# Chunks of the first half of the first gated layer in engine loops, and a wait for the delta scan's state signal written ahead of the first merge chunk's load

## Chip, core and metric

The kernel runs on one core of one Trainium2 chip. The metric is the device time of one execution in microseconds (us), as the median of several executions. Lower is better.

## The reference, cut to what matters

Two blocks run one after the other on 528 tokens (16 meta tokens and 512) of width 1024. The part that the change touches is the first of the two gated layers of the first block, and a load in its mixing part:

```python
for l in range(DEPTH):                                   # DEPTH = 1
    h = h + 0.5 * swiglu(rmsnorm(h, ffn1_norm[l]), ffn1_w_gate[l], ffn1_w_up[l], ffn1_w_down[l])
    u = rmsnorm(h, mix_norm[l])
    (c_q, c_kv, k_rope, g_q, g_k, g_v, g_b, g_a, g_z,
     gate_mla, gate_gdn) = jnp.split(u @ w_in[l], split_points, axis=-1)
    y_mla = mla(...) @ w_mla_o[l]
    y_gdn = gated_deltanet(...) @ w_gdn_o[l]             # a scan over 9 chunks of 64 tokens with a state
    merged = jax.nn.sigmoid(gate_mla) * y_mla + jax.nn.sigmoid(gate_gdn) * y_gdn
    h = h + merged @ w_out[l]
    h = h + 0.5 * swiglu(rmsnorm(h, ffn2_norm[l]), ...)

def swiglu(x, w_gate, w_up, w_down):                     # hidden width D_FF = 2816
    return (jax.nn.silu(x @ w_gate) * (x @ w_up)) @ w_down
```

A second block, an attention layer of three branches, follows and is not touched.

## The kernel before, in words

All large weights come through one stream of chunks. A chunk is up to 128 x 2048 numbers (1 MB); `STREAM` lists the runs of chunks by name, and `n` numbers them through the whole kernel. `RAW`, `WHI` and `WLO` have two slots each, and chunk n uses slot n % 2. Each engine has its own part of the work on a chunk and its own program:

- SyncE (SP) loads chunk n into `RAW` (L592) once `lo_rdy` (printed as weights_lo_ready) says that the slot's chunk before, n - 2, is split.
- ScalarE (ACT) makes the rounded part, `WHI` (L1540), of chunk n + 1 while TensorE multiplies chunk n.
- VectorE (DVE) makes the rest, `WLO` = `RAW` - `WHI` (L2123), of chunk n + 1.
- TensorE (PE) multiplies: for each block three products, `WHI` by the high part of the tokens, `WLO` by the high part, `WHI` by the low part (L743, L744, L745), 264 columns each.
- VectorE and ScalarE turn the result into the hidden layer: DVE `SILU` (L2349), ACT `TANH` (L1676), DVE `SILU` (L2351), DVE `GF` (L2356, which frees the PSUM banks: `evac`), DVE `GF` (L2359), ACT `GH` (L1678), DVE `GL` (L2361).

A gated layer f runs in two halves of 11 hidden blocks. "f1u0" is the gate and up product of the first half of the first layer (11 chunks, numbers 0 to 10), "f1d0" its down product (8 chunks), then "f1u1" and "f1d1". In f1u0 one chunk is 96 matmuls on TensorE (8 x 2 x 2 x 3), in f1d0 it is 66. Two PSUM halves alternate: the matmuls of chunk n wait until chunk n - 2 is read (`evac` at n - 1) and until `WLO` of chunk n is there.

The function `stream(eng, name, body, straight, first)` writes one engine's program for a run. With `straight=True` each chunk's instructions are written out. Otherwise `first` chunks (2 if it is the kernel's first run) are written out, the next ones stand once, two chunks per pass, in a loop of the engine (`eng.Fori`, L406), and what is left over is written out. In a loop the chunk number `n` that the body gets is not a Python integer but an expression over the loop's register, so every semaphore count and address that depends on it is computed by register instructions, and a test such as `isinstance(n, int)` is false. That f1d0 stands in a loop on TensorE and SyncE, and that f2u0, f2d0, f2u1, the second layer's runs, and the merge chunks "mg" stand in loops, is so before and after.

The merge chunks: "mg" is a run of 16. SyncE's program for it starts at its first chunk in a loop (first=0: seven passes of two, two chunks written out). The delta scan is the loop over `NCH` = 9 chunks behind L2860; `st_rdy` is its semaphore, raised by 2 at L2861 when the state is cleared, and by one for each half of a new state. Engines take the waits of their own program in order: what stands behind a waiting instruction on an engine waits too.

The functions that the diff touches, and what calls them:

Of the kernel before, what the change touches and what calls it, by code (L numbers as in the profile page):

```python
# [49 lines left out]
START = {}  # L50
# [29 lines left out]
def build(nc, io):  # L80
# [216 lines left out]
    def halves(ap):  # L297
# [39 lines left out]
    st_rdy, ws_ps, vn_rdy, sa_ps, o_ps, o_ev = (sem(x) for x in (  # L337
        "state_ready", "ws_in_psum", "v_new_ready", "state_add_in_psum", "delta_o_in_psum",
        "delta_o_ready"))
# [42 lines left out]
    def chunk_width(name, parity):  # L382
        if name == "mg":
            return SLOT if parity == 0 else SLOT // 2
        return WIDTH[name]

    def stream(eng, name, body, straight=False, first=0):

        n0, count = START[name], COUNT[name]
        at_ = ORDER.index(name)
        after = chunk_width(ORDER[at_ + 1], 0) if at_ + 1 < len(ORDER) else 0
        head = 2 if n0 == 0 else first

        def one(j):
            n = n0 + j
            body(n, j, n // 2, n % 2, chunk_width(name, (j + 1) % 2) if j + 1 < count else after)

        if straight:  # L400
            head = count
        for j in range(head):
            one(j)
        trips = (count - head - 1) // 2
        if trips > 1:
            with eng.Fori(0, trips) as i:  # L406
                for s in range(2):
                    n = n0 + head + s
                    body(2 * i + n, 2 * i + head + s, i + n // 2, n % 2,
                         chunk_width(name, (head + s + 1) % 2))  # L410
            done = head + 2 * trips
        else:
            done = head
        for j in range(done, count):
            one(j)
# [156 lines left out]
    @block.sync  # L572
    def _(sp):
        sp.dma_start(COL[:, :], io["cols"]).then_inc(col_ld, 16)
        for i in range(2):
            sp.dma_start(first_half(RAW, i), io["f1u0"][0].rearrange("p (a b) -> p a b", a=2)[
                :, :, i * KD // 2 * P:(i + 1) * KD // 2 * P]).then_inc((w0_ld, raw_ld[0])[i], 16)
        load_h(sp, 1)
        sp.dma_start(TAB[:, 0:TABS["cos"]], io["tabs"][:, 0:TABS["cos"]]).then_inc(ones_ld, 16)

        def load(name):
            def body(n, j, turn, slot, nxt):
                if isinstance(n, int) and n == 0:
                    return
                if isinstance(n, int) and n - 2 in SEVEN:
                    sp.wait_ge(p_lo, 7 * SEVEN[n - 2] + 7)
                elif not isinstance(n, int) or n >= 2:
                    sp.wait_ge(lo_rdy, n)
                w = chunk_width(name, (n - START[name]) % 2 if isinstance(n, int) else
                                (slot - START[name]) % 2)  # L590
                src = io[name][j] if name != "mg" else io["mg"][j, :, 0:w]
                sp.dma_start(RAW[:, slot, 0:w], src).then_inc(raw_ld[slot], 16)  # L592
                if isinstance(n, int) and n == 1:
                    sp.dma_start(RELB[:, :], io["rel"]).then_inc(tab_ld, 16)
                    sp.dma_start(TAB[:, TABS["cos"]:], io["tabs"][:, TABS["cos"]:]).then_inc(tab_ld, 16)
            return body

        def spread_rows():

            sp.wait_ge(gt_d, 6)  # L600
            sp.dma_start(io["rows"][0], RW[B8, 0, :]).then_inc(row_st, 16)
            sp.dma_start(io["rows"][1], RW[A8, 1, :]).then_inc(row_st, 16)
            sp.wait_ge(row_st, 32)
            for i, (t, landed) in enumerate(((EU, kx_ld), (QX, qx_ld))):
                if i:
                    sp.wait_ge(kn_ps, 4)
                for p in range(2):
                    sp.dma_start(pair_rows(t)[CH * p:CH * (p + 1), :, :],
                                 bass.AP(io["rows"].tensor, (NH * i + p) * NROW, [[0, CH], [2 * NROW, 4], [1, NROW]]))\
                        .then_inc(landed, 16)  # L610

        for name in ORDER[:-1]:
            stream(sp, name, load(name), straight=name in ("f1u0", "f1u1"), first=2 if name in ("f1d0", "f1d1") else 0)
            if name == "z":
                spread_rows()
        n0 = START["wo2"]
        for j in range(2):
            load("wo2")(n0 + j, j, 0, (n0 + j) % 2, 0)

        for j in range(2, 4):  # L620
            load("wo2")(n0 + j, j, 0, (n0 + j) % 2, 0)
        for j in range(4):
            sp.wait_ge(evac, n0 + j + 1)
            sp.dma_start(io["out"][2 * j:2 * j + 2].rearrange("k p t -> p k t"),
                         H[:, 2 * j:2 * j + 2, N_META:T1]).then_inc(out_st, 16)
        sp.wait_ge(out_st, 64)
# [111 lines left out]
    def _(pe):  # L738
# [109 lines left out]
        def ffn(f, c0, w):  # L848
            hi, lo = parts(3 * f)
            gh, gl = hidden(f)  # L850
            for half in range(2):
                def up(n, j, turn, slot, nxt):
                    if isinstance(n, int) and n == 0:
                        warm_up()
                        first_chunk(hi, lo)
                        return
                    if seven(n):
                        seven_products(n)
                        if ends_run(n):
                            pe.sem_inc(mm_done, n + 1 - SEVEN_FIRST[n])  # L860
                        return
                    pe.wait_ge(lo_rdy, n + 2)
                    if not isinstance(n, int) or n >= 2:
                        pe.wait_ge(evac, n - 1)
                    if isinstance(n, int) and n == START["f2u0"] + 1:

                        pe.wait_ge(rstd_rdy, TURN[3])
                    for k in range(KD):
                        pe.wait_ge(ul_rdy, KD * ROUND[3 * f] + k + 1)
                        if isinstance(n, int) and (n, k) in ((1, 3), (START["f2u0"], 3)):  # L870
                            square_sums(3 * f)
                        for which in range(2):
                            for b, (a, m, c) in enumerate(pieces(w)):
                                last = mm3(PS[:, 4 * slot + 2 * which + b, c:c + m], slot,
                                           (which * KD + k) * P, hi[:, k, a:a + m], lo[:, k, a:a + m],
                                           k == 0, k == KD - 1)
                    last.then_inc(mm_done, 1)

                def down(n, j, turn, slot, nxt):
                    pe.wait_ge(lo_rdy, n + 2)  # L880
                    pe.wait_ge(evac, n - 1)
                    if last_down(f, half, j):
                        down_by_halves(n, slot, gh, gl)
                        return
                    for k in range(FHALF):
                        pe.wait_ge(gl_rdy, (2 * f + half) * FHALF + k + 1)
                        for b, (a, m, c) in enumerate(pieces(w)):
                            last = mm3(PS[:, 4 * slot + b, c:c + m], slot, k * P, gh[:, k, a:a + m],
                                       gl[:, k, a:a + m], k == 0, k == FHALF - 1)
                    last.then_inc(mm_done, 1)  # L890

                if f == 0 and half == 1:
                    pe.wait_ge(rev_rdy, 1)
                stream(pe, f"f{f + 1}u{half}", up, straight=f == 0, first=2)
                if f == 0 and half == 0:
                    relative_rows()
                stream(pe, f"f{f + 1}d{half}", down, first=0 if f else 2)
# [326 lines left out]
        for g in range(NB // SIDE):  # L1224
            for lv in range(LEVELS):
                for x in range(SIDE):
# [10 lines left out]
                    for r in range(UB):  # L1237
                        u = (SIDE * g + x) * UB + r
# [9 lines left out]
                for x in range(SIDE if lv else 0):  # L1248
# [4 lines left out]
                    for r in range(UB):  # L1253
                        u = b * UB + r
# [8 lines left out]
            for x in range(SIDE):  # L1263
# [3 lines left out]
                for r in range(UB):  # L1267
                    u = b * UB + r
# [101 lines left out]
        n = START["wv"]  # L1370
# [130 lines left out]
        n = START["wt"]  # L1501
# [26 lines left out]
    def _(act):  # L1528
# [125 lines left out]
        def ffn(f, c0, w):  # L1654
            TANH, SILU, GF = staging(f)
            for half in range(2):
# [31 lines left out]
                        act.wait_ge(evac, n + 1)  # L1688
                        high(1, j)

                stream(act, f"f{f + 1}u{half}", up, straight=f == 0, first=2)
                stream(act, f"f{f + 1}d{half}", down, straight=f == 0 or half == 1)

        def only_weights(n, j, turn, slot, nxt):
# [69 lines left out]
        n = START["uq"]  # L1764
# [151 lines left out]
        n = START["z"]  # L1916
# [63 lines left out]
        n = START["wv"]  # L1980
# [128 lines left out]
    def _(dve):  # L2109
# [216 lines left out]
        def ffn(f, c0, w):  # L2326
            gh, gl = hidden(f)
            TANH, SILU, GF = staging(f)
            for half in range(2):
# [58 lines left out]
                        if f == 0:  # L2388
                            low(1, j)

                stream(dve, f"f{f + 1}u{half}", up, straight=f == 0, first=0 if half else 2)
                if f == 0 and half == 0:
                    dve.wait_ge(rev_ps, 1)
                    TS(REV, PS[0:16, 7, 0:383], -1.0, None, ALU.mult).then_inc(rev_rdy, 1)
# [939 lines left out]
```

## Time and profile before

| | |
|---|---|
| time of three runs, median | 1569.19 us (1568.25 to 1571.32) |
| time of the profiled execution | 1561.85 us |
| its span, first to last instruction | 1560.2 us |
| mean granted TensorE clock | 0.993 of full |
| TensorE busy | 1524.6 us (98%) |
| VectorE busy | 955.0 us (61%) |
| ScalarE busy | 593.9 us (38%) |

The profile is of one execution, by the hardware's own records. PE stands for TensorE's matmuls, PEld for its weight loads, which overlap them; DVE is VectorE, ACT ScalarE, POOL GpSimd, SP SyncE. A q behind an engine's name is its sequencer, the part that waits, branches, computes registers and issues transfers; its instructions are not counted as busy. L743 is line 743 of the kernel. In a row of the timeline the first number is the start in us from the span's start, the second the duration; brackets give the engine's idle time before and what ended it.

### The profile page before, as it was taken

Reading aid. Unit: us, or ns where it says so; the run is one execution under the profiler, and the core shown is the slowest. Engines: PE = TensorE matmul, PEld = TensorE weight load, DVE = VectorE, ACT = ScalarE, POOL = GpSimd, SP = SyncE. Lnnn points to the kernel's source line nnn. Section 1 sums busy time; section 2 is a strip of 40 time slices with the busy share of each in tenths; the row PEclk is TensorE's granted clock in tenths of the full one; section 3 lists DMA queues with packets and bytes.
Section 4 is the critical chain, followed back from the end, with each engine's and each line's share of the span. In section 5 each row is a group of like instructions: output and inputs, shape, how many; then the busy total and the mean of one; then the engine's idle time right before and its main releaser. Section 6 shows DMA issues by size and latency. Waiting matters only on the chain.

```text
span 1560.2 us, 30264 instructions
## 1 busy us (share of the span) xinstructions
PE 1524.6 (98%) x12676; PEld 1338.6 (86%) x12676; DVE 955.0 (61%) x1528; ACT 593.9 (38%) x968; POOL 127.6 (8%) x124
## 2 busy tenths in 40 slices
PE   9999999999999999999999989999999989999998
PEld 8999999999997789988888878888888877776777
DVE  6546588855389776555445666634666565557872
ACT  6222356632255562042232322222322144446960
POOL 0000000000001640500000000000000000000410
PEclk9999999999999999999999999999999999999999
DMA  6222223246332200012224243433442353211001
GB/s 242 82 101 75 96 96 109 92 116 150 95 76 69 62 3 31 4 43 75 100 81 164 93 162 121 137 103 125 149 147 81 101 217 135 71 52 55 2 10 73
DMA packets 27683, 147.92 MB, mean 95 GB/s; under 512 B 2928, under 2 KB 3328, under 8 KB 16944
## 3 DMA queue, kind: packets, MB, share of 16 engines
q1 hardware_dynamic: 21616, 122.50, 22.9%
q0 software_dynamic: 5424, 22.68, 5.4%
q8 instruction: 88, 1.44, 0.4%
q10 hardware_dynamic: 528, 1.08, 0.2%
q14 instruction: 27, 0.22, 0.0%
HBM read 140.97 MB, written 5.27 MB: 94 GB/s over the span
## 4 chain that ended last, share of the span: by engine, by line
PE 90%; DVE 4%; ACT 3%; issue 1%; DMA 1%; DVEq 0%; SPq 0%; ACTq 0%; POOLq 0%
PE PS L743 22%; PE PS L744 22%; PE PS L745 22%; PE PS L843 2%; PE PS L845 2%; PE PS L844 2%; PE PS L1260 1%; PE PS L1195 1%; PE PS L1245 1%; PE PS L1155 1%; PE PS L1068 1%; PE PS L1258 1%; ACT PB L1898 1%; PE PS L779 1%; PE PS L1169 1%
## 5 line engine op out<-in xcount | busy, mean ns | idle before, releaser
L1540 ACT ACTIVATE WHI<-RAW 128x2048 fp32r<-128x2048 f32 (+3 forms) x113 | 189.4, 1676 | 277.6 <-PE PS L745 273.6
L2123 DVE TENSOR_TENSOR WLO<-RAW,WHI 128x2048 fp32r<-128x2048 f32 (+3 forms) x113 | 225.9, 1999 | 66.1 <-ACT WHI L1540 65.3
L743 PE MATMUL PS<-UH,WHI 128*128 128x264 f32 (+1 forms) x736 | 227.6, 309 | 2.1 <-DVE WLO L2123 2.1
L744 PE MATMUL PS<-UH,WLO 128*128 128x264 f32 (+1 forms) x736 | 226.3, 307 | 0.0
L745 PE MATMUL PS<-UL,WHI 128*128 128x264 f32 (+1 forms) x736 | 226.0, 307 | 0.0
L743 PE MATMUL PS<-UHS,WHI 128*128 128x512 f32 x520 | 205.5, 395 | 5.2 <-DVE WLO L2123 5.2
L745 PE MATMUL PS<-ULS,WHI 128*128 128x512 f32 x520 | 203.4, 391 | 0.0
L744 PE MATMUL PS<-UHS,WLO 128*128 128x512 f32 x520 | 203.3, 391 | 0.0
L743 PEld LDWEIGHTS PS<-UH,WHI 128*128 128x128 f32 x736 | 139.2, 189 | 9.1 <-DVE WLO L2123 2.5
L744 PEld LDWEIGHTS PS<-UH,WLO 128*128 128x128 f32 x736 | 139.2, 189 | 6.4 <-issue 0.2
L745 PEld LDWEIGHTS PS<-UL,WHI 128*128 128x128 f32 x736 | 138.9, 189 | 6.3
L743 PEld LDWEIGHTS PS<-UHS,WHI 128*128 128x128 f32 x520 | 98.3, 189 | 27.7 <-issue 7.1
L745 PEld LDWEIGHTS PS<-ULS,WHI 128*128 128x128 f32 x520 | 98.2, 189 | 20.8
L744 PEld LDWEIGHTS PS<-UHS,WLO 128*128 128x128 f32 x520 | 98.4, 189 | 20.0 <-issue 0.2
L744 PE MATMUL PS<-GH,WLO 128*128 128x264 f32 x352 | 100.2, 285 | 0.0
L745 PE MATMUL PS<-GL,WHI 128*128 128x264 f32 x352 | 100.0, 284 | 0.0
L743 PE MATMUL PS<-GH,WHI 128*128 128x264 f32 x352 | 99.8, 284 | 0.0
L1676 ACT ACTIVATE TANH<-SILU 128x512 f32<-128x512 f32 (+1 forms) x33 | 21.0, 637 | 191.4 <-DVE SILU L2349 191.4
L843 PE MATMUL PS<-FH,WHI 128*128 128x264 f32 x308 | 87.8, 285 | 0.1
L845 PE MATMUL PS<-FL,WHI 128*128 128x264 f32 x308 | 87.3, 283 | 0.0
L844 PE MATMUL PS<-FH,WLO 128*128 128x264 f32 x308 | 87.2, 283 | 0.0
L2381 DVE SCALAR_TENSOR_TENSOR H<-PS,H 128x528 f32<-128x528 f32 (+2 forms) x31 | 21.6, 697 | 96.1 <-PE PS L745 96.1
(474 smaller groups left out, 3256.2 us busy)
## 6 DMA issues: line engine op xcount, KB each, us to landing
RAW<-in_f2u SPq DMA_DIRECT2D x22, 1024.0 KB, 4.9
RAW<-in_f1u SPq DMA_DIRECT2D x21, 1024.0 KB, 4.8
ADA<-in_ada POOLq DMA_DIRECT2D x24, 512.0 KB, 4.8
RAW<-in_f1d SPq DMA_DIRECT2D x16, 704.0 KB, 4.1
RAW<-in_f2d SPq DMA_DIRECT2D x16, 704.0 KB, 4.1
RAW<-in_wi SPq DMA_DIRECT2D x10, 1024.0 KB, 4.9
RAW<-in_w SPq DMA_DIRECT2D x8, 1024.0 KB, 5.1
RAW<-in_mg SPq DMA_DIRECT2D x8, 1024.0 KB, 4.9
```

The lines of the kernel that those rows point to most:

```text
L743: mm(out, WHI[:, slot, c:c + w], hi, start=first, stop=False)
L744: mm(out, WLO[:, slot, c:c + w], hi, start=False, stop=False)
L745: return mm(out, WHI[:, slot, c:c + w], lo, start=False, stop=last)
L779: out = mm(PS[:, 2 * which + b, c:c + m], stationary[:, 0, (which * KD + k) * P:(which * KD + k + 1) * P], moving[:, k, a:a + m], start=fi ...
L843: mm(out, whi[:, ks], hi, start=starts and k == 0, stop=False, skip_group_check=True)
L844: mm(out, wlo[:, ks], hi, start=False, stop=False, skip_group_check=True)
L845: last = mm(out, whi[:, ks], lo, start=False, stop=ends, skip_group_check=True)
L1068: last = mm(scores(i, p, k0, k1), q, KH[0:96, h, k0:k1], start=True, stop=True)
L1540: A(WHI[:, slot, 0:w], RAW[:, slot, 0:w], ACT.Copy).then_inc(hi_rdy, 1)
L1676: A(TANH[:, slot, 0:w], SILU[:, slot, 0:w], ACT.Tanh, scale=0.5).then_inc(tanh_rdy, 1)
L2123: TT(WLO[:, slot, 0:w], RAW[:, slot, 0:w], WHI[:, slot, 0:w].bitcast(f32), ALU.subtract).then_inc(lo_rdy, 1)
L2381: STT(h, psum(4 * slot, w), 0.25, h, ALU.mult, ALU.add)\
```

## The change

Two edits. In SyncE's load of a chunk a wait for `st_rdy` >= 2 is added under the condition that the chunk number is an integer and is that of the first merge chunk. And the run f1u0 is no longer straight on SyncE, TensorE, ScalarE and VectorE; f1u1 stays straight.

```diff
@@ load(name) of SyncE
                 elif not isinstance(n, int) or n >= 2:
                     sp.wait_ge(lo_rdy, n)
+                if isinstance(n, int) and n == START["mg"]:
+                    sp.wait_ge(st_rdy, 2)
                 w = chunk_width(name, (n - START[name]) % 2 if isinstance(n, int) else
@@ SyncE
-            stream(sp, name, load(name), straight=name in ("f1u0", "f1u1"), first=2 if name in ("f1d0", "f1d1") else 0)
+            stream(sp, name, load(name), straight=name == "f1u1", first=2 if name in ("f1d0", "f1d1") else 0)
@@ TensorE
-                stream(pe, f"f{f + 1}u{half}", up, straight=f == 0, first=2)
+                stream(pe, f"f{f + 1}u{half}", up, straight=f == 0 and half == 1, first=2)
@@ ScalarE
-                stream(act, f"f{f + 1}u{half}", up, straight=f == 0, first=2)
+                stream(act, f"f{f + 1}u{half}", up, straight=f == 0 and half == 1, first=2)
@@ VectorE
-                stream(dve, f"f{f + 1}u{half}", up, straight=f == 0, first=0 if half else 2)
+                stream(dve, f"f{f + 1}u{half}", up, straight=f == 0 and half == 1, first=0 if half else 2)
```

The lines behind L588 move by two in the changed kernel. How the programs of three engines change:

SyncE, at the start of the merge chunks, in the changed kernel (RAW<-in_mg is the load of a merge chunk; QX<-rows is a transfer of the delta part, ahead of it):

```order
L610 DMA QX<-rows 64x4x576
L406 UNCONDITIONAL_BRANCH
L406 ISA
L594 ISA [waits weights_lo_ready]
L594 DMA RAW<-in_mg 128x2048
L588 REGISTER_ALU
L594 ISA [waits weights_lo_ready]
L594 DMA RAW<-in_mg 128x1024
L406 REGISTER_ALU
L406 COMPARE_AND_BRANCH
```

The rows of before are these same ten with L592 for L594 and L608 for L610. The loads wait for weights_lo_ready alone in both.

TensorE in f1u0, the edge between chunks 1 and 2, before:

```order
L744 MATMUL PS<-UH_79,WLO 128x264
L745 MATMUL PS<-UL_80,WHI 128x264
L743 MATMUL PS<-UH_79,WHI 128x264 [waits normed_lo_ready,chunk_evacuated,weights_lo_ready]
L744 MATMUL PS<-UH_79,WLO 128x264
L745 MATMUL PS<-UL_80,WHI 128x264
```

and in the changed kernel (the edge, then the end of the loop's body and the first matmul of chunk 10 behind it):

```order
L747 MATMUL PS<-UL_80,WHI 128x264
L406 UNCONDITIONAL_BRANCH
L406 ISA
L866 REGISTER_ALU [waits weights_lo_ready]
L745 MATMUL PS<-UH_79,WHI 128x264 [waits normed_lo_ready,chunk_evacuated]
...
L406 REGISTER_ALU
L406 COMPARE_AND_BRANCH
L745 MATMUL PS<-UH_79,WHI 128x264 [waits normed_lo_ready,chunk_evacuated,weights_lo_ready]
```

The matmuls and their waits are the same; a branch and register instructions stand at the edge, and the 192 matmuls of two chunks, with as many weight loads, stand between the loop's head and its branch.

VectorE in f1u0, one chunk as it stands written out for each of chunks 2 to 10 before:

```order
L2123 TENSOR_TENSOR WLO<-RAW,WHI 128x2048 [waits chunk_multiplied,weights_hi_ready]
L2349 TENSOR_TENSOR SILU_74<-PS,KEEP 128x528 [waits hidden_ready,rstd_ready,chunk_multiplied]
L2351 SCALAR_TENSOR_TENSOR SILU_74<-TANH_73,SILU_74 128x528 [waits tanh_ready]
L2356 TENSOR_TENSOR GF_75<-SILU_74,PS 128x528 [waits hidden_lo_ready,silu_ready]
L2359 TENSOR_TENSOR GF_75<-GF_75,KEEP 128x528 [waits chunk_evacuated]
L2361 TENSOR_TENSOR GL<-GF_75,GH 128x528 [waits hidden_hi_ready]
```

and the loop's first chunk in the changed kernel:

```order
L406 ISA
L492 REGISTER_ALU [waits weights_hi_ready]
L2125 TENSOR_TENSOR WLO<-RAW,WHI 128x2048 [waits chunk_multiplied]
L2346 REGISTER_ALU
L2349 REGISTER_ALU [waits rstd_ready,chunk_multiplied]
L2351 TENSOR_TENSOR SILU_74<-PS,KEEP 128x528 [waits hidden_ready]
L2353 SCALAR_TENSOR_TENSOR SILU_74<-TANH_73,SILU_74 128x528 [waits tanh_ready]
L2358 TENSOR_TENSOR GF_75<-SILU_74,PS 128x528 [waits hidden_lo_ready,silu_ready]
L2361 TENSOR_TENSOR GF_75<-GF_75,KEEP 128x528 [waits chunk_evacuated]
L2363 ISA [waits hidden_hi_ready]
L2363 TENSOR_TENSOR GL<-GF_75,GH 128x528
```

The six operations of a chunk keep their order; a register instruction or a wait of its own stands ahead of some of them.

## Rows read from the trace of the kernel before

**Rows 1.** The page: busy time, the chain that ended last, the instruction queue.

```profile
PE 1524.6 (98%) x12676; PEld 1338.6 (86%) x12676; DVE 955.0 (61%) x1528; ACT 593.9 (38%) x968; POOL 127.6 (8%) x124
...
q8 instruction: 88, 1.44, 0.4%
...
PE 90%; DVE 4%; ACT 3%; issue 1%; DMA 1%; DVEq 0%; SPq 0%; ACTq 0%; POOLq 0%
```

**Rows 2.** Busy time by windows: f1u0 and f1d0 (window us, busy us, instructions).

```profile
21.20:138.40 117.20, 117.20 (x971) 116.92 (x969) 61.86 (x63) 34.66 (x36) 0.00 (x0) 1.00 0.26 90
139.30:203.90 64.60, 64.60 (x532) 64.60 (x533) 40.39 (x45) 20.36 (x21) 6.25 (x2) 1.00 0.26 89
```

**Rows 3.** All waits of weight loads, 21.2 to 204 us (total us, times, longest).

```profile
PEld PS L743 <- issue: 0.6, 1, 0.6
PEld PS L766 <- issue: 0.2, 1, 0.2
```

**Rows 4.** Timeline of VectorE in f1u0, one chunk.

```profile
45.87 0.71 DVE L2349 TENSOR_TENSOR SILU<-PS,KEEP 128x528 f32<-128x528 f32 x1 [3.17 <-PE PS L745]
...
50.20 0.71 DVE L2361 TENSOR_TENSOR GL<-GF,GH 128x528 fp32r<-128x528 f32 x1 [0.71 <-ACT GH L1678]
52.01 2.29 DVE L2123 TENSOR_TENSOR WLO<-RAW,WHI 128x2048 fp32r<-128x2048 f32 x1 [1.10 <-ACT WHI L1540]
57.46 0.71 DVE L2349 TENSOR_TENSOR SILU<-PS,KEEP 128x528 f32<-128x528 f32 x1 [3.16 <-PE PS L745]
```

**Rows 5.** Timeline of ScalarE in f1u0, the same chunk.

```profile
46.61 0.65 ACT L1676 ACTIVATE TANH<-SILU 128x528 f32<-128x528 f32 x1 [6.23 <-DVE SILU L2349]
49.52 0.65 ACT L1678 ACTIVATE GH<-GF 128x528 fp32r<-128x528 f32 x1 [2.26 <-DVE GF L2359]
50.07 1.90 ACT L1540 ACTIVATE WHI<-RAW 128x2048 fp32r<-128x2048 f32 x1
```

**Rows 6.** Timeline of VectorE in f2u1, in a loop before and after.

```profile
1102.53 0.69 DVE L2349 TENSOR_TENSOR SILU<-PS,RSTD 128x512 f32<-128x512 f32 x1 [1.32 <-PE PS L745]
...
1107.07 0.69 DVE L2361 TENSOR_TENSOR GLS<-GF,GHS 128x512 f32 x1 [0.93 <-ACT GHS L1678]
1108.75 2.29 DVE L2123 TENSOR_TENSOR WLO<-RAW,WHI 128x2048 fp32r<-128x2048 f32 x1 [0.99 <-ACT WHI L1540]
```

**Rows 7.** Sequencers at the loops' line, whole kernel, then 150 to 190 us.

```profile
L406 SPq COMPARE_BRANCH  x34: 40/45/54, 146.4 to 1334.1; - x34
L406 PEldq COMPARE_BRANCH  x25: 76/208/240, 169.3 to 1230.4; - x25
L406 DVEq COMPARE_BRANCH  x18: 50/56/68, 741.8 to 1183.3; - x18
L406 ACTq COMPARE_BRANCH  x17: 40/45/54, 741.0 to 1182.5; - x17
...
L406 PEldq COMPARE_BRANCH  x2: 76/158/240, 169.3 to 185.4; - x2
```

**Rows 8.** DMA queue of TensorE's instructions (packets, MB, share): 155 to 187, 21 to 139 us.

```profile
q8 instruction: 1, 0.02, 0.2%
...
q8 instruction: 7, 0.11, 0.4%
```

**Rows 9.** DMA issues: KB each, us from issue to landing.

```profile
RAW<-in_f1u SPq DMA_DIRECT2D x21, 1024.0 KB, 4.8
RAW<-in_mg SPq DMA_DIRECT2D x8, 1024.0 KB, 4.9
COL<-in_cols SPq DMA_DIRECT2D x1, 94.0 KB, 2.3
```

**Rows 10.** Timelines around the delta scan: SyncE, VectorE, ScalarE.

```profile
599.07 115.65 SPq L592 DMA_DIRECT2D RAW<-in_mg  x4
...
660.89 0.27 DVE L2860 MEMSET SV<- 128x256 f32 x1
...
682.70 1.90 ACT L1540 ACTIVATE WHI<-RAW 128x2048 fp32r<-128x2048 f32 x1
```

**Rows 11.** Timeline of TensorE in f2u0 behind an idle stretch.

```profile
919.71 0.77 PE L743 MATMUL PS<-UHS,WHI 128*128 128x512 f32 x1 [5.25 <-DVE WLO L2123]
920.27 0.63 PE L744 MATMUL PS<-UHS,WLO 128*128 128x512 f32 x1
920.70 0.63 PE L745 MATMUL PS<-ULS,WHI 128*128 128x512 f32 x1
...
925.38 0.39 PE L744 MATMUL PS<-UHS,WLO 128*128 128x512 f32 x1
925.61 0.40 PE L745 MATMUL PS<-ULS,WHI 128*128 128x512 f32 x1
```

**Rows 12.** The same place by windows: the clock stands behind the counts.

```profile
919.60:925.80 6.20, 6.09 (x15) 4.84 (x16) 4.38 (x7) 2.17 (x3) 0.53 (x1) 0.54 0.71 254
925.80:935.00 9.20, 9.20 (x42) 7.59 (x41) 4.12 (x4) 1.49 (x2) 0.53 (x1) 1.00 0.48 171
```

## The prediction, made before the changed kernel was run

> **What bounds the kernel.** I read the page first. TensorE is busy for 98% of the span, and 90% of the chain that ended last is TensorE's own work [rows 1]. So a change counts only where it delays or hastens a matmul. Then I looked at the stretch that the change rewrites. In the 117.20 us of f1u0 TensorE is busy for all 117.20 us, at full clock, through 971 instructions, which is 0.121 us for each [rows 2]. One chunk of 96 matmuls is therefore 11.6 us. The list of waits says the same from the other side: over f1u0 and f1d0 the weight loads wait 0.6 us and 0.2 us, once each, and for no other engine [rows 3]. The reader is to see that f1u0 is a pure TensorE stretch, in which the other three engines have slack. The question is how much slack, and what a loop costs against it.
>
> **The first edit, the wait.** Its condition asks for an integer chunk number. SyncE takes the merge chunks from the first one in a loop, where the number is an expression over a register, so the condition is false when the program is written. The listing in the section on the change bears this out: the load of the first merge chunk waits for weights_lo_ready alone, as before. Cost 0, because nothing is added.
>
> I also price the case that it were there. The first merge load is issued at 599.07 us. The signal comes when the state is cleared, at 660.89 + 0.27 = 661.2 us. ScalarE first reads the chunk at 682.70 us [rows 10]. The load would land 4.9 us behind its issue [rows 9], at 666.1 us, 16.6 us before it is wanted. Behind it on SyncE stand only later merge loads, which wait for this chunk to be split. So a real wait would cost 0 too.
>
> **The second edit, TensorE.** Chunks 2 to 9 become four passes of two chunks; chunks 0, 1 and 10 stay written out. Added are a loop entry and, per pass, register instructions and a branch, of which three are taken. A taken branch on TensorE's sequencer takes about 0.21 to 0.24 us, one that falls through 0.076 us [rows 7]. The nearest stretch that already is a loop on TensorE is f1d0, with the same matmul shape. It spends 64.60 us of 64.60 us busy on 532 instructions, again 0.121 us each [rows 2], and the list of waits has no entry for its edges [rows 3] (the 0.6 us stands before f1d0's first matmul, at the one small matmul of the relative rows). What hides the branch there is that the sequencer is ahead of the array: it branched back at 169.3 us [rows 7], while the matmuls of four chunks, 4 x 66 x 0.121 = 32.0 us from 139.3 us, end at 171.3 us. That is 2.0 us ahead. Branch and register work of perhaps 0.4 us per pass fit into it. Cost 0; without that cover it would be 4 x 0.4 = 1.6 us.
>
> **VectorE.** In f1u0 one chunk on VectorE runs from `SILU` at 45.87 us to the end of `WLO` at 52.01 + 2.29 = 54.30 us, and then VectorE is idle for 3.16 us until TensorE has finished [rows 4]. `WLO` of the next chunk is thus ready 3.2 us before TensorE can use it. What do the register instructions cost? The second layer's f2u1 runs the same operations in a loop. From the start of `SILU` to the end of `GL` it takes 1107.07 + 0.69 - 1102.53 = 5.23 us [rows 6], against 50.20 + 0.71 - 45.87 = 5.04 us written out [rows 4]. From the start of `GL` to the start of `WLO` it is 1.68 us [rows 6] against 1.81 us [rows 4]. So a loop costs 0.2 us per chunk, and with the branch of 0.056 us [rows 7] at most 0.5 us. It is hidden under 3.2 us. With the cover gone it would be 8 x 0.2 to 8 x 0.5 us, 1.6 to 4 us.
>
> **ScalarE and SyncE.** ScalarE waits 6.23 us for VectorE ahead of `TANH` [rows 5]; its own loop branch takes 0.045 us [rows 7]. Cost 0. SyncE issues the next load when `WLO` ends, for example at 54.30 us; it lands 4.8 us later [rows 9], at 59.1 us. That load is of the chunk after next in the same slot, which ScalarE reads two chunk periods behind 50.07 us [rows 5], at 73.3 us. The slack is 14 us, and SyncE adds a few register instructions and a 0.045 us branch [rows 7], below 0.3 us together. Cost 0.
>
> **The sum.** 0 + 0 + 0 + 0 = 0 us on the profiled execution's own 1561.85 us. That execution was 7.3 us faster than the median of the three runs shown, 1569.19 us, so I forecast a median of about 1569.2 us. About 0.2%, 3.1 us, is what a measurement of this kernel can tell from no change; its three runs alone differ by 3.1 us.
>
> **The unknown: where a branch jumps to.** The new body on TensorE is 192 matmuls with 192 weight loads. Instructions arrive in packets over a queue of their own: seven of them in the 118 us of f1u0 [rows 8], in which some 971 matmuls and as many weight loads run, so a packet carries roughly 2 x 971 / 7 = 277 instructions, and the new body of 384 is more than one packet and can touch three. The largest looped body before, f1d0's of 264, can touch two; in its two passes one packet came [rows 8] and no matmul waited [rows 3]. So a branch back over one packet border is free, and over two is not shown. Priced from rows: the nearest row for a small transfer is 2.3 us for 94 KB [rows 9]. One packet fetched again is covered but for 2.3 - 2.0 = 0.3 us, or 0.9 us over three branches. Two, one behind the other, leave 4.6 - 2.0 = 2.6 us, 7.8 us in all. The upper bound is three packets, 6.9 - 2.0 = 4.9 us, plus a lower clock behind so long a stop: behind 5.25 us of idleness the granted clock was 0.54 for 6 us [rows 12], and 13 matmuls started 0.43 us apart instead of 0.23 us [rows 11], 2.6 us lost. That is 3 x 7.5 = 22 us. I take 0, since f1d0, the nearest stretch, shows 0. The lower bound is 0 as well: TensorE has no idle time here to win back.
>
> The Trainium skill, "Runtime: NRT & Kernel Launch", section "Instruction fetch mechanics", speaks against this edit: it says that a taken branch whose target is outside the present two pages of instructions forces a fetch before work goes on. It gives a page as 256 instructions, by which the body of 384 would reach a third page in about half of all placements (estimate: (384 - 256) / 256). The same section gives TensorE room for 2048 instructions, by which the whole body would stay. Nothing in the trace of before decides between the two; what hangs on it is the second rival below.
>
> **The rivals.**
> - The loop is hidden, no change: 1569.2 us, likeliest. For it: f1d0 and the slack of each engine.
> - TensorE's instructions are fetched again at each branch back: 1569.2 + 7.8 = 1577 us, with 22 us more as the worst. It decides once a stop is longer than the 2.0 us lead by 1 us per branch, 3 us in all. For it: the body is larger than any looped one before. Against it: no looped stretch shows a fetch at a branch.
> - The register work breaks a cover: if VectorE's real slack at a loop's head were gone, 1569.2 + 4 = 1573 us. Against it: 3.2 us of slack against 0.5 us.
> - Faster: the instructions of six chunks are no longer written out and fetched, and all later packet borders move. In the stretches of short matmuls this could remove stops; "issue" is 1% of the chain [rows 1], some 16 us, and a fifth of it would be 3 us: 1566 us. Nothing in the rows ties those stops to packets.
> - The wait is really there: 0 us as priced, so it makes no difference to the result.
>
> **Chances.** No change 0.84 (with the wait real or not), fetched again 0.07, cover broken 0.04, faster 0.05. Of these the fetch case falls below 0.2% in some of its range, but a drift between measurements can add as much to either side. So faster 0.06, within 0.2% 0.83, slower 0.11. The range is 1564 to 1575 us: it holds the likeliest case with the distance of single executions, and leaves out most of the fetch case.
>
> **What would show it.** In the profile of the changed kernel: the window of f1u0 still about 117 us and TensorE fully busy in it; no wait of a weight load near 57, 81 and 104 us, where the branches back are taken (chunk 3 ends at 57.46 us [rows 4], and a pass is 23.2 us); VectorE's idle time ahead of `SILU` down from 3.2 us to about 2.9 us; SyncE's first merge load still near 599 us; seven or fewer packets on the instruction queue in f1u0. I am wrong if weight loads in f1u0 wait for "issue" by 1 us or more at the branches, with extra packets there, or if `WLO` comes to end TensorE's waits.

## The result: 0.7% faster, where no change was forecast

The changed kernel takes 1558.66 us (median of 5 runs, 1557.85 to 1560.81), the kernel before 1569.19 us beside it (5 runs, 1567.99 to 1572.21). The ratio is 0.993 with a 95% interval of 0.9915 to 0.9945: 10.5 us less, and outside the predicted range of 1564 to 1575 us.

The profiled executions differ by less: 1557.85 us now against 1561.85 us before. So 4.0 us of the gain lie between the two traces, and the rest must lie in executions of before that the first trace doesn't show. One execution of before in the second comparison below, at 1893 us and a granted clock of 0.743, was disturbed and is left out everywhere.

### The profile after: the rewritten stretch

The page of the changed kernel (busy time, instruction queue), to be held against [rows 1]:

```profile
PE 1519.9 (98%) x12676; PEld 1334.2 (86%) x12676; DVE 955.3 (61%) x1528; ACT 593.6 (38%) x968; POOL 127.0 (8%) x124
...
q8 instruction: 84, 1.38, 0.4%
```

Its f1u0 and f1d0 by windows, as in [rows 2]:

```profile
21.00:138.40 117.40, 117.40 (x972) 117.09 (x971) 61.88 (x64) 34.67 (x36) 0.00 (x0) 1.00 0.25 89
138.90:203.70 64.80, 64.80 (x533) 64.68 (x533) 40.65 (x46) 20.34 (x21) 6.26 (x2) 1.00 0.26 89
```

All waits of weight loads from 21.2 to 204 us, as in [rows 3]:

```profile
PEld PS L745 <- issue: 0.6, 1, 0.6
PEld PS L768 <- issue: 0.2, 1, 0.2
```

VectorE's timeline over one chunk edge in the new loop, as in [rows 4]:

```profile
45.78 0.71 DVE L2351 TENSOR_TENSOR SILU<-PS,KEEP 128x528 f32<-128x528 f32 x1 [3.14 <-PE PS L747]
...
50.41 0.71 DVE L2363 TENSOR_TENSOR GL<-GF,GH 128x528 f32 x1 [0.94 <-ACT GH L1680]
52.09 2.29 DVE L2125 TENSOR_TENSOR WLO<-RAW,WHI 128x2048 fp32r<-128x2048 f32 x1 [0.97 <-ACT WHI L1542]
57.28 0.71 DVE L2351 TENSOR_TENSOR SILU<-PS,KEEP 128x528 f32<-128x528 f32 x1 [2.90 <-PE PS L747]
```

TensorE's instruction packets from 21 to 139 us (packets, MB, share of the DMA engines' time), as in [rows 8], where there were seven:

```profile
q8 instruction: 3, 0.05, 0.1%
```

The reader is to see that f1u0 is what it was: busy throughout, no new wait, VectorE's idle time down from 3.2 to 2.9 us. The loop itself gained and cost nothing. Three packets come instead of seven, since none comes in the later passes.

### Where the time went: a load, TensorE's instructions, and its clock

Followed operation by operation on VectorE, the two traces run alike, within 0.4 us, to 467 us. Then the profile before loses time at three places where the granted clock was half for 3.4 us each (from 468.0, 553.3 and 563.5 us), and the profile after at none of them. The first place by windows (the clock stands behind the counts), before:

```profile
464.00:467.90 3.90, 1.96 (x16) 1.75 (x15) 3.77 (x6) 1.91 (x1) 0.00 (x0) 1.00 0.00 0
468.00:471.30 3.30, 3.30 (x17) 3.30 (x16) 3.17 (x5) 0.00 (x0) 0.00 (x0) 0.50 0.53 161
```

and after:

```profile
464.00:467.90 3.90, 1.95 (x16) 1.74 (x15) 3.85 (x6) 1.91 (x1) 0.00 (x0) 1.00 0.00 0
468.00:471.30 3.30, 3.30 (x29) 3.30 (x29) 3.17 (x6) 0.00 (x0) 0.00 (x0) 1.00 0.49 159
```

TensorE did the same ahead of both, idle for half of 3.9 us, and the clock fell to 1.2 GHz in the one and stayed at 2.4 GHz in the other. Such short falls come and go without the change: the profile of e1 below, the same instructions as before, has of the three only the one at 553.7 us, and that of e3, which has the whole gain, has two (552.4 and 562.6 us). They explain the 4.0 us between the two profiles and not the 10.5 us between the medians.

The larger part is in the delta part's inverse (its ladder of small matmuls, L1245 to L1260 before, L1247 to L1262 after, 585 to 660 us). Weight loads' waits from 590 to 630 us, before:

```profile
PEld PS L1258 <- issue: 0.8, 3, 0.5
PEld PS L1245 <- issue: 0.2, 1, 0.2
```

After, both rows are gone. "issue" means that the engine waited for nothing that the profile shows. The longest of these stops in the chain of before:

```profile
605.40 0.36 issue
605.76 0.25 PE PS L1258 x2
```

What it waited for is seen in the DMA views. The first merge load of before leaves at 599.07 us [rows 10]. From 601.6 to 603.4 us before, the queues hold (q1 carries the loads, q8 TensorE's instructions):

```profile
q1 hardware_dynamic: 92, 0.68, 90.7%
```

and from 603.4 to 604.6 us:

```profile
q8 instruction: 1, 0.02, 5.0%
q1 hardware_dynamic: 7, 0.00, 0.3%
```

In the ladder TensorE uses up one packet in some 3.75 us. That is about 256 instructions (an estimate: 1474 matmuls in 43.75 busy us after the change, and as many weight loads, make 253 in 3.75 us). In the trace's raw records of before the packets start at 595.13, 598.88 and then 603.50 us, 4.6 us apart, right where the load's last large packet is through. After that TensorE stops at 605.4 us. In the changed kernel the load leaves at 596.31 us and its data run from 597.33 to 600.86 us; the packets start at 596.97 and 600.74 us, 3.77 us apart: one just ahead of the load's data, one as their last bytes come in.

What ties the stop to the late packet is the time between them. Five profiles have such a packet (before, e1, e4, e8, e9), and in each TensorE starts again 1.30 to 1.41 us behind its landing: at 605.76 us behind 604.46 us in before, at 605.73 us behind 604.43 us in e9. A load beside the ladder is not enough by itself: in the profiles after and of e2, e3 and e7 the load runs there too (in e3 from 599.18 to 602.76 us, almost where it runs before), but the packets fall ahead of it and at its end, and TensorE has no stop for "issue".

What such a stop can bring on is seen in the profile of the wait alone (first experiment), whose instructions are those of before. Windows of TensorE from 600 us (busy time and matmuls, granted clock, DMA share, GB/s):

```profile
600.00:604.00 4.00, 4.00 (x145) 1.00 0.78 262
604.00:608.00 4.00, 3.56 (x123) 1.00 0.02 4
608.00:612.00 4.00, 4.00 (x88) 0.54 0.01 4
612.00:620.00 8.00, 8.00 (x156) 0.50 0.01 2
620.00:629.00 9.00, 9.00 (x177) 0.51 0.01 3
```

and the chain at its stop:

```profile
604.99 0.45 issue
605.44 0.25 PE PS L1260 x2
```

The same stretch after the change:

```profile
604.00:608.00 4.00, 4.00 (x145) 1.00 0.02 4
609.00:628.00 19.00, 17.84 (x603) 1.00 0.01 4
```

against, in the profile of the wait alone:

```profile
609.00:628.00 19.00, 19.00 (x362) 0.50 0.01 3
```

The clock falls 2.9 us behind the stop. TensorE then works at 1.2 GHz from 608.3 us for 20.5 us; half of that, 10.2 us, is lost. That is the size of the gain.

**Theory E.** The first merge load, 1 MB, holds up one packet of TensorE's instructions; TensorE stops; in most executions the clock then halves for 20 to 27 us. The change moves the borders of the instruction packets, since TensorE's program is 1150 instructions shorter ahead of this place (6 chunks of 192 matmuls and weight loads, less a few for the loop). The loops have no other part in it. **Rivals:** a drift between measurements (B), and something in the loop or the program's length itself (F).

### The profile page after: what moved, and what is told of

The parts are those of the page before. It is cut to its first block, busy times and chain, and to the rows that moved or that the text cites. A ratio compares the mean times of both kernels' runs of the same rounds, so it can differ in the third digit from the quotient of the medians.

```text
span 1556.2 us, 30392 instructions
## 1 busy us (share of the span) xinstructions
PE 1519.9 (98%) x12676; PEld 1334.2 (86%) x12676; DVE 955.3 (61%) x1528; ACT 593.6 (38%) x968; POOL 127.0 (8%) x124
## 4 chain that ended last, share of the span: by engine, by line
PE 87%; DVE 7%; ACT 3%; issue 2%; DMA 1%; POOL 1%; DVEq 0%; SPq 0%; ACTq 0%; POOLq 0%
PE PS L745 22%; PE PS L746 22%; PE PS L747 22%; PE PS L845 2%; PE PS L847 2%; PE PS L846 2%; PE PS L1262 1%; PE PS L1197 1%; PE PS L1157 1%; PE PS L1247 1%; PE PS L1260 1%; ACT PB L1900 1%; PE PS L781 1%; DVE WLO L2125 1%; PE PS L1070 1%
```

## Experiments

Each was timed beside the kernel before, the first four on one chip, the next four on a second, the last three on a third. Beside the median each row tells in how many executions the mean granted clock was below 0.993. The traces tie this to the long half-clock stretch: the five profiles that have it (e1, e4, e8, e9, e10) are at 0.988 to 0.991, the eight others at 0.993 to 0.998. The changed kernel itself had it in 0 of 5.

| run | median us | ratio to before (95%) | with the stretch |
|---|---|---|---|
| before, chip of 1 to 4 | 1571.87 | | 21 of 23 |
| e1 wait only | 1569.21 | 0.9979 (0.995 to 1.0008) | 9 of 12 |
| e2 loops only | 1557.82 | 0.9924 (0.9896 to 0.9952) | 0 of 6 |
| e3 TensorE's loop only | 1558.16 | 0.9926 (0.9898 to 0.9954) | 0 of 6 |
| e4 the other three loops | 1569.75 | 0.9975 (0.995 to 1.0) | 9 of 12 |
| before, chip of 5 to 8 | 1569.15 | | 19 of 21 |
| e5 real wait | 1559.13 | 0.9944 (0.9926 to 0.9963) | 0 of 8 |
| e6 loops and real wait | 1558.37 | 0.9938 (0.9914 to 0.9962) | 0 of 6 |
| e7 before, packet borders moved | 1558.76 | 0.9945 (0.9922 to 0.9967) | 0 of 8 |
| e8 after, borders moved back | 1564.45 | 0.9963 (0.9941 to 0.9985) | 6 of 12 |
| before, chip of 9 to 11 | 1569.69 | | 26 of 29 |
| e9 after, load 2.7 us later | 1570.64 | 1.0017 (0.9997 to 1.0037) | 12 of 12 |
| e10 real wait, 3.0 us stop | 1572.86 | 1.0026 (1.001 to 1.0041) | 12 of 12 |
| e11 real wait, 0.2 us stop | 1560.34 | 0.9946 (0.9926 to 0.9965) | 0 of 12 |

In e1, e4 and e8 the executions with the stretch take 1567.0 us and more, those without it 1561.9 us and less.

### e1: the wait alone

```diff
+                if isinstance(n, int) and n == START["mg"]:
+                    sp.wait_ge(st_rdy, 2)
```

> Only the first edit of the change: the wait on the state signal under its condition, all loops as before. The condition is never true where the program is written, so this is the program of before with its line numbers moved. Theory A (the gain of 10.5 us comes from the second edit, through stretches in which TensorE's granted clock fell to half before and not after): no change, about 1569 us, and the granted clock near 0.99 with falls between 460 and 570 us. Theory B (the gain is a drift between measurements or between chips and not the change's): this kernel shows a gain like the change's, or the kernel beside it comes out near 1559 us. A wait that acted would show as a first merge load behind 661 us instead of near 599 us.

Measured: 1569.21 us, no difference that can be told, and a mean clock of 0.990 as theory A said. But the falls were not where it said: between 460 and 570 us there is one, of 3.4 us, and the long one starts at 608.3 us. So this edit does nothing, and the gain is no drift, for e2 and e3 beside it have it. One thing was new: 3 of 12 executions of this program took 1557.7 to 1559.9 us. The same instructions run with and without the loss.

### e2: the loops alone

```diff
-                if isinstance(n, int) and n == START["mg"]:
-                    sp.wait_ge(st_rdy, 2)
```

> Only the second edit: f1u0 in loops on all four engines, no wait written. Theory A: the whole change, about 1559 us, f1u0 still 117 us long. Theory B: no gain against the kernel before on the same chip.

Measured: 1557.82 us, as theory A said of the time. The second edit is the whole change.

### e3 and e4: TensorE's loop alone, and the other three

```diff
@@ e3: TensorE alone
-                stream(pe, f"f{f + 1}u{half}", up, straight=f == 0, first=2)
+                stream(pe, f"f{f + 1}u{half}", up, straight=f == 0 and half == 1, first=2)
@@ e4: SyncE, ScalarE and VectorE as in the change, TensorE as before
```

> f1u0 in a loop on TensorE alone; SyncE, ScalarE and VectorE written out as before. Theory C (TensorE's shorter program moves the borders of its instruction packets, and with them short stops in the stretches of weak activity behind 460 us): the whole gain, about 1559 us. Theory D (what matters is a shift by a fraction of a us in when the small operations fall against the clock's own rhythm): some value between 1557 and 1572 us that need not go with the sum of the parts.

> f1u0 in loops on SyncE, ScalarE and VectorE; TensorE written out as before. Theory C: no gain, about 1569 us, because TensorE's instruction stream is that of before. Theory D: any value between 1557 and 1572 us. If both this and the TensorE loop alone stay at 1569 us, the gain needs both.

Measured: 1558.16 us and 1569.75 us. TensorE's loop is the gain, the other three have no part in it. That is theory C's forecast, though its stops lie near 605 us and not right behind 460 us. D, by which any shift of small operations matters, allowed any value and is not excluded by these two times; the stop is what speaks against it. In the profile of e4 the packets start at 595.32 and 601.22 us, 5.9 us apart around a load at 596.57 us, and TensorE stops: a weight load waits 1.1 us, and the clock is half from 603.3 us for 27.3 us. The profile of e3 has neither the stop nor the long stretch.

### e5 and e6: the wait made real

Put ahead of the run of merge chunks, outside the loop, in the kernel before (e5) and in the changed one (e6):

```diff
             if name == "z":
                 spread_rows()
+                sp.wait_ge(st_rdy, 2)
```

> The kernel before, f1u0 written out, with one line added: SyncE waits for the state signal of the delta scan ahead of the run of merge chunks, so that the first merge load can't leave before about 661 us. Theory E (in the kernel before the first merge load, 599 to 604 us, holds up packets of TensorE's instructions; TensorE stops for 0.3 to 0.7 us in the inverse's short matmuls, and in most executions its granted clock then halves for 20 to 27 us): no stops between 600 and 615 us, no long half-clock stretch, about 1558 us, as fast as the whole change. Rival F (the gain of the TensorE loop has to do with the length of its program, and not with the load): no gain, about 1570 us. My prediction held this wait to be worth 0.

> The changed kernel with the same wait ahead of the run of merge chunks. Theory E: the change has taken the loss away already, so nothing is added: about 1558 us. Rival F: no further gain either; but if half-clock stretches of another cause are left, it stays where the change is.

Measured: 1559.13 us and 1558.37 us. SyncE's timeline in e5:

```profile
660.42 0.38 SPq L592 DMA_DIRECT2D RAW<-in_mg  x1
```

TensorE's instruction packets in e5 start 3.74, 3.72 and 3.74 us apart from 594.74 to 605.94 us. With TensorE's program as it was, and f1u0 written out, moving one load away gives the whole gain. Rival F falls. And the two ways don't add up, as theory E said: both take away the same loss.

### e7 and e8: the packet borders moved without the loop

141 raises of a semaphore that nothing reads, in f1u1 of the kernel before; 137 in the changed kernel. By the traces 11 waits that stood as instructions of their own are gone with them, so the programs are 130 and 126 instructions longer. They bring the borders, modulo 256 instructions, to where the other kernel has them.

```diff
@@ seven_products of TensorE (e8: 13 if c % 2 else 12)
+                for _ in range((13 if c < 9 else 12) if i == 0 else 0):
+                    pe.sem_inc(padding, 1)
```

> The kernel before with 130 more instructions in TensorE's program, in f1u1: raises of a semaphore that nothing reads, 11 or 12 for each of 11 chunks. This puts the borders of TensorE's instruction packets, 256 instructions each, where the changed kernel has them behind f1u0 (its program is 1150 instructions shorter there, 4 x 256 + 126), but has no loop and loads as before. Theory E in the form that the place of the packet borders against the load decides: about 1558 us and no stops at 600 to 615 us. Rival F (a loop, or a shorter program, is what helps): about 1570 us.

> The changed kernel with 126 such instructions more in f1u1, so that the packet borders behind it stand where they were before the change. Theory E: the loss comes back, about 1569 us with stops near 600 us and a half-clock stretch of 20 to 27 us, although f1u0 is in loops. Rival F: the gain stays, about 1558 us.

Measured: 1558.76 us for the longer program of e7, in none of 8 executions with the stretch. So a program that is longer by 130 instructions is as fast as one that is shorter by 1150. In e8 the loss is back in 6 of 12 executions, and its profile has it:

```profile
PEld PS L1265 <- issue: 1.0, 1, 1.0
```

e8's median lies between the levels, 4.7 us under the 1569.15 us of before, where I expected it. It is a mixture of two kinds of execution and not a third level; the loss came in half of them, in e1 in three quarters. Why it is less often was not settled.

### e9: the load moved, the program left alone

```diff
             if name == "z":
                 spread_rows()
+                sp.wait_ge(t_rdy, 9)
```

> The changed kernel with the first merge load about 2.3 us later: SyncE waits for the ninth update of the inverse (t_rdy >= 9) ahead of the run. TensorE's program is not touched. In the profile after, the load leaves at 596.3 us, its packets run from 597.3 to 600.9 us, and TensorE's instruction packets start at 597.0 and 600.7 us, just ahead of it and just behind. Theory E: the load's packets now run from about 599.6 to 603.2 us, the instruction packet due at 600.7 us starts about 2 us late, TensorE stops for some 1 us, and the loss comes back in most executions, about 1568 us. Rival F: no effect, about 1558 us, for TensorE's program is that of the change.

Measured: 1570.64 us, with the stretch in 12 of 12. SyncE's timeline, the wait for instructions, and the queues from 601.6 to 603.4 us and from 603.4 to 604.6 us in e9:

```profile
599.02 0.38 SPq L594 DMA_DIRECT2D RAW<-in_mg  x1
```

```profile
PEld PS L1248 <- issue: 1.5, 1, 1.5
```

```profile
q1 hardware_dynamic: 89, 0.65, 85.7%
...
q8 instruction: 1, 0.02, 5.0%
q1 hardware_dynamic: 7, 0.01, 1.9%
```

The load left 2.7 us later than in the changed kernel, and its data ran from 600.03 to 603.91 us. The packet due 3.8 us behind that of 597.59 us started at 603.47 us, 2.1 us late, and the whole gain was gone, with all of the change's code in place. The same collision can be had from either side: by moving the borders or by moving the load.

### e10 and e11: a stop without a load

On top of e5, where no load is near, 24 or 6 raises in TensorE's program inside the ladder:

```diff
+                for _ in range(24 if (g, lv) == (0, 4) else 0):
+                    pe.sem_inc(padding, 1)
```

> The kernel before with the wait ahead of the merge loads (as e5), so that no load is near, and 24 raises of an unread semaphore in TensorE's program ahead of the fifth level of the inverse in its first group of units, 51 ns each: a stop of about 1.2 us that has nothing to do with a load or a packet. Theory G (a stop of about 1 us there is enough for the granted clock to halve for 20 to 27 us): about 1568 us, a half-clock stretch behind 605 us in most executions. Rival H (the half clock needs the load's or the packets' own work, or several stops): about 1560 us, the stop alone on top of e5.

> The same with 6 raises, a stop of about 0.3 us, as the shortest ones seen in the kernel before. Theory G: too short in most executions; 1559 us, with some executions near 1568 us at most. If even this gives 1568 us in most executions, the stretch is on the edge of halving and any stop tips it.

e10's stop came out longer than I expected, 3.0 us instead of 1.2 us:

```profile
PEld PS L1249 <- issue: 3.0, 1, 3.0
```

The trace has the reason. The raises took 51 ns each, as expected, but from the first to the last start 3.6 us passed (number, duration in ns, first and last start), 0.15 us for each:

```profile
L1229 PEldq EVENT_SEMAPHORE  x24: 51/51/51, 605.5 to 609.1; - x24
```

Its windows of TensorE:

```profile
600.00:608.60 8.60, 6.29 (x216) 1.00 0.02 4
608.70:632.00 23.30, 22.84 (x428) 0.50 0.01 2
```

Measured: 1572.86 us, in 12 of 12 executions with the stretch. Against e5, on another chip on which before took 0.5 us less, that is 13.7 us: up to 3 us for the stop and about 11 us for the half clock. So a stop without a load is enough if it is of 3.0 us, and the clock is what makes it dear. For the 1.2 us that theory G named it was not tried. e11's stop showed 0.2 us in the waits view, and the kernel took 1560.34 us with no stretch in 12 executions, as forecast. Between 0.2 and 3.0 us this pair says nothing; in the traces where packets were late, single stops of 0.6, 1.0, 1.1 and 1.5 us stood ahead of the stretch, and four of at most 0.5 us, in the profile of before, did not bring it. That a stop of this size brings the stretch on without a load beside it is therefore argued from its place and from the runs without it, and not shown by itself.

## Why the prediction was wrong, point by point

- **The first edit does nothing as written: right.** e1 shows it. **"So a real wait would cost 0 too": wrong**, though the sum doesn't use it, as the wait isn't there. I asked when the load lands and when it is wanted, 16.6 us apart, and priced it at 0. I did not ask what else was on the DMA engines while it ran. e5 measured what that wait is worth: 10 us less.
- **TensorE's term of the sum, "Cost 0", with "The lower bound is 0 as well: TensorE has no idle time here to win back": the step that failed.** I looked for what the shorter program gains in f1u0 alone. Its effect lies nearly 500 us behind it: the moved packet borders take away TensorE's stop at 605 us and the 20.5 us at half clock behind it, 10.2 us in e1's profile. Measured against before, e3 (TensorE's loop alone) is 13.7 us faster and e7 (borders moved, no loop) 10.4 us.
- **"Cost 0" for TensorE, VectorE, ScalarE and SyncE inside f1u0: right.** The window, the waits and the slack of 2.9 us came as told.
- **The unknown of the branch back: settled at 0.** In the first pass of the new body, 31.8 to 55.0 us, two instruction packets started (33.25 and 48.50 us), so the body seems to reach over two borders; how far ahead of its use a packet starts, and with it where the first border lies, no trace shows. None came in the later passes, and nothing waited. By the Trainium skill, "Runtime: NRT & Kernel Launch", section "Instruction fetch mechanics", a branch out of a window of two pages forces a fetch. If the body does reach over two borders, the trace disagrees for TensorE; in either case it agrees with the 2048 instructions that the same section gives TensorE.
- **The sum's last step, "that execution was 7.3 us faster than the median of the three runs shown, so I forecast a median of about 1569.2 us": the second failure.** I carried those 7.3 us over as a constant. They were part of the loss that the change takes away. The profiled execution of before was one of the few without the long stretch (across the three later comparisons, 66 of 73 executions of before had it), so the trace I argued from did not contain it. What the trace did contain was its cause.
- **The rival "faster" had the mechanism and missed the size.** It said that all later packet borders move and that this could remove stops in the stretches of short matmuls, worth 3 us with a chance of 0.05 (0.06 with drift). The stops that vanished in the profile between 590 and 630 us are 1.0 us in all. The rival was mis-sized because I priced the stops and not what they do to the clock, 10.2 us. I also wrote that nothing in the rows ties those stops to packets; the DMA queues by window, from 599 to 604 us, would have.
- **What would show it.** None of the signs that I named for being wrong came. They all looked at f1u0, where the edit is, and the effect was 500 us behind it.

## What to carry to other kernels

When the profiled execution is faster or slower than the median by more than the runs spread, find out what the others have that it lacks, before forecasting a change against either. An engine's instructions come in over DMA too: a large load that is hidden by its own deadline can still stop an engine that runs through its program fast, so hold it until the short instructions are done, as e5 did. A change of program length moves every later packet border; a gain that comes from that is luck of placement, and the wait that keeps the load away (e5, e6) gives the same time without it.

## What the runs showed of the hardware that I had not expected

- A 1 MB load whose packets ran from 600.1 to 603.5 us held back a 16 KB packet of TensorE's instructions until 603.50 us; in e9 the load's data ran to 603.91 us and the packet started at 603.47 us. What the two share on the way is not shown. The Trainium skill, "Runtime: NRT & Kernel Launch", section "Instruction fetch mechanics", calls the cost of crossing a 16 KB border mostly hidden. That holds in f1u0, where a packet lasts some 15 us, and in the ladder without a load near (e5); it did not hold in the ladder under a load.
- The granted clock's fall outlasts its cause. TensorE was idle for 0.45 us at 605 us in e1, was at 1.2 GHz from 608.3 to 628.8 us, and stayed busy all the while; in e10 the stretch was 23.9 us long.
- Whether a given stop is followed by it differs between executions of one program (9 of 12 in e1, 6 of 12 in e8). The Trainium skill, "TensorE: Matmul & The Clock Gate", section "What's actually happening", calls the moment at which the clock is decided free-running against the program, so that the same kernel meets it at different places. The runs agree with that; none of them shows the mechanism itself.
- Raises of a semaphore in TensorE's program, 24 in a row, stopped it for 3.0 us, where the sequencer's 51 ns for such an instruction made me expect 1.2 us. They start 0.15 us apart; what fills the 0.1 us between two of them is not shown.
